# The head of a one-layer encoder block on one core: loads of x and of the first weights in another order, the z projection in pieces around the transposes, roots and low parts on other engines

## The reference

```python
def rmsnorm(x, g):
    y = x * lax.rsqrt(jnp.mean(x * x, axis=-1, keepdims=True) + EPS) * g

h = rmsnorm(x, norm_mix_g)
proj = h @ w_in        # attention q|k|v, DeltaNet q|k|v|z|a|b, two gates
ya = swa_sink_attention(aq, ak, av, ...)
yb = gated_deltanet(bq, bk, bv, bz, ba, bb, ...)   # conv + SiLU on q, k, v; SiLU(z) on the output
x = x + (sigmoid(ga) * (ya @ w_up_a) + sigmoid(gb) * (yb @ w_up_b)) @ w_out
x = x + memory_cross_attention(rmsnorm(x), rmsnorm(mem), ...)
x = x + hierarchical_moe(rmsnorm(x), ...)          # 32 experts, top 2 of the best group
return rmsnorm(x, norm_final_g)
```

## Time and profile before

| | us |
|---|---|
| median of 3 runs | 805.44 (804.22 to 806.6) |
| the profiled execution, its own time | 806.24 |
| its span | 804.4 |
| busy in the span: PE, PEld | 748.4, 598.3 |
| busy in the span: DVE, ACT, POOL | 341.6, 256.1, 300.7 |

### The profile page before, as it was taken

One profiled execution on the slowest core, in us unless ns is written; L12 is line 12 of the kernel. 1 busy time (PEld: TensorE's weight loads), 2 busy tenths in 40 slices (PEclk: granted clock), 3 DMA queues, 4 the chain that ended last, 5 costly groups with the idle time before them and its releaser, 6 DMA issues.

```text
span 804.4 us, 14079 instructions
## 1 busy us (share of the span) xinstructions
PE 748.4 (93%) x5523; PEld 598.3 (74%) x5523; DVE 341.6 (42%) x805; ACT 256.1 (32%) x462; POOL 300.7 (37%) x346
## 2 busy tenths in 40 slices
PE   5999999999999999999999999979999999988784
PEld 5887788788878877888888887857767776665551
DVE  6466643285684861435415333651222112211125
ACT  5343232361633767322305255511111111111012
POOL 2774525441520452254444254333333333322111
PEclk9999999999999999999999999999999999999998
DMA  9956742510220522474385294499999999999975
GB/s 250 162 110 124 218 124 53 104 42 13 53 53 20 136 56 53 98 216 96 83 176 169 60 320 183 180 358 375 390 385 389 390 393 387 380 386 387 390 300 219
DMA packets 74346, 166.60 MB, mean 207 GB/s; under 512 B 18838, under 2 KB 46310, under 8 KB 66344
## 3 DMA queue, kind: packets, MB, share of 16 engines
q1 hardware_dynamic: 65856, 150.34, 58.9%
q0 software_dynamic: 5392, 9.61, 3.6%
q10 hardware_dynamic: 3032, 5.74, 2.3%
HBM read 156.98 MB, written 16.97 MB: 216 GB/s over the span
## 4 chain that ended last, share of the span: by engine, by line
PE 58%; DMA 26%; DVE 9%; issue 2%; POOL 2%; ACT 1%; SPq 1%; ACTq 0%; DVEq 0%; POOLq 0%
DMA arena<-in_w_exp_up 24%; PE bank L1075 13%; PE bank L1077 12%; PE bank L1076 12%; PE bank L1068 12%; PE bank L1424 3%; DMA arena<-y_half 1%; PE bank L1434 1%; PE bank L1116 1%; DVE rows L1864 1%; DVE rows L1863 1%; PE bank L1226 1%; DVE h_lo L1836 1%; DVE hT L1908 1%; DMA rt<-in_norm_ffn_g 1%
## 5 line engine op out<-in xcount | busy, mean ns | idle before, releaser
L876 POOL TENSOR_TENSOR ring_low<-ring,w_high 128x512 fp32r<-128x512 f32 (+1 forms) x64 | 81.4, 1272 | 117.2 <-ACT w_high L1516 113.1
L1075 PE MATMUL bank<-h_hi,w_high 128*128 128x512 f32 x296 | 119.5, 404 | 0.0
L1076 PE MATMUL bank<-h_lo,w_high 128*128 128x512 f32 x296 | 115.8, 391 | 0.0
L1424 PEld LDWEIGHTS bank<-arena,hT 128*64 128x64 f32 x1728 | 96.6, 136 | 24.7 <-issue 12.5
L1424 PE MATMUL bank<-arena,hT 128*64 128x128 f32 x1728 | 100.7, 274 | 8.7 <-DMA arena<-in_w_exp_up 6.7
L876 POOL TENSOR_TENSOR w_low<-ring,w_high 128x512 fp32r<-128x512 f32 x56 | 75.9, 1355 | 59.1 <-ACT w_high L1516 54.9
L2182 DVE SCALAR_TENSOR_TENSOR rt<-rt,bank 128x128 f32<-128x128 f32 x32 | 9.2, 288 | 175.3 <-ACT rt L1749 175.3
L1516 ACT ACTIVATE w_high<-ring 128x2048 fp32r<-128x2048 f32 (+1 forms) x32 | 58.7, 1836 | 58.5 <-PE bank L1077 39.3
L1077 PE MATMUL bank<-h_hi,ring_low 128*128 128x512 f32 x168 | 66.6, 396 | 0.0
L1075 PEld LDWEIGHTS bank<-h_hi,w_high 128*128 128x128 f32 x296 | 55.7, 188 | 14.5 <-issue 3.5
L1076 PEld LDWEIGHTS bank<-h_lo,w_high 128*128 128x128 f32 x296 | 55.7, 188 | 11.0
(11 more groups left out here) (330 smaller groups left out, 1313.8 us busy)
## 6 DMA issues: line engine op xcount, KB each, us to landing
arena<-in_w_exp_gate SPq DMA_DIRECT2D x27, 1024.0 KB, 13.3
arena<-in_w_exp_up SPq DMA_DIRECT2D x27, 1024.0 KB, 17.0
arena<-in_w_exp_down SPq DMA_DIRECT2D x27, 1024.0 KB, 19.2
ring<-in_w_in SPq DMA_DIRECT2D x33, 512.0 KB, 6.6
ring<-in_w_exp_gate SPq DMA_DIRECT2D x5, 1024.0 KB, 13.8
ring<-in_w_exp_up SPq DMA_DIRECT2D x5, 1024.0 KB, 17.3
ring<-in_w_exp_down SPq DMA_DIRECT2D x5, 1024.0 KB, 20.5
xres<-in_x SPq DMA_DIRECT2D x8, 512.0 KB, 7.2
```

Of the source, the lines that this page charges most:

```text
L876: after(pool.tensor_tensor(low, full, high, ALU.subtract), w_lo if kk == KD - 2 else step["pool"])
L1075: pe.matmul(o, l_hi, r_hi, start=(n == 0), stop=False)
L1076: pe.matmul(o, l_hi, r_lo, start=False, stop=False)
L1424: ins = pe.matmul(bank[CAP * half:CAP * half + CAP, 1, P * n:P * n + P], xgT[:, x, kk, :], w[:, kk, P * half:P * half + P], start=(kk == 0 ...
```

## The change

- SP issues the loads as x tile 0, first half of the lead, x tile 1, second half of the lead, x tiles 2 and 3, chunks 1 and 2.
- The first two z jobs become four: `("zp",0)`, which does high by high of tile 0 between the transposes of tiles 0 and 1; `("zp",1)`, the rest of tile 0 and high by high and high by low of tile 1, between the transposes of tiles 1 and 2; `("z",0,0)`, low by high of tile 1; `("z",0,1)`, all of tiles 2 and 3 in six passes of 8 matmuls, the low parts of h last. The first three share a bank.
- The root of tile 1 moves from DVE to POOL (six instructions with a power in place of twelve). DVE makes the roots of tiles 2 and 3 after the gains of tile 1.
- POOL no longer waits for the diagonals. Its `h_lo` of tile 0 comes between the lead's low parts; `h_lo` of tile 1 and the low part of chunk 1 come next, `h_lo` of tiles 2 and 3 after those. ACT makes the high part of chunk 1 after `h_hi` of tile 1.
- DVE makes `h_lo` of tiles 0 and 1 as each tile's gains are done, of 2 and 3 after all gains.

```diff
+    turned = [[("hT", "mix", t, q) for q in range(2)] for t in range(NT)]
+    jobs = [("vec",)] + turned[0] + [("zp", 0)] + turned[1] + [("zp", 1)] + turned[2] + turned[3]
...
@@ sync
-            for t in range(NT):
+            def load_x(t):
                 sp.dma_start(xres[:, t, :], x[0, t * P:(t + 1) * P, :]).then_inc(x_in[t], 16)
+            load_x(0)
...
                     sp.dma_start(lead_dst[:, 0:4], lead_src[:, 0:4]).then_inc(lead_in, 16)
+                    load_x(1)
...
+                if n == 0:
+                    load_x(2)
+                    load_x(3)
...
@@ gpsimd
-            pool.wait_ge(diag_ready, NT)
             for n in range(4):
                 s = slice(n * CHUNK_W // 4, (n + 1) * CHUNK_W // 4)
+                if n == 1:
+                    v, y, y2 = var[:, 1:2], rstd[:, 1:2], newton[:, 1:2]
+                    pool.wait_ge(squared, 2)
+                    after(pool.tensor_scalar(v, squares[:, 1:2], 1.0 / D, EPS, ALU.mult, ALU.add))
+                    after(pool.tensor_tensor(y, v, neg_half, ALU.pow))
...
+                    after(pool.tensor_tensor(y, y, y2, ALU.mult), mix_rstd)
+                if n == 2:
+                    low_of_hT("mix", 0)
...
-            for t in range(NT):
+            low_of_hT("mix", 1)
+            low_part(1)
+            for t in range(2, NT):
                 low_of_hT("mix", t)
...
@@ tensor
+                    order = {("zp", 0): [(0, h_hi, 0)], ("zp", 1): [(0, h_lo, 0), (0, h_hi, 1), (1, h_hi, 0), (1, h_hi, 1)], ("z", 0, 0): [(1, h_lo, 0)],
+                             ("z", 0, 1): [(2, h_hi, 0), (2, h_hi, 1), (3, h_hi, 0), (3, h_hi, 1), (2, h_lo, 0), (3, h_lo, 0)]}[job]
...
@@ scalar
+                    square(0)
+                    lead_high(0, lead_in, 16, lead_hi)
+                    square(1)
+                    lead_high(1, chunk_in[0], 32, w_hi)
+                    high_of_hT(phase, 0)
+                    square(2)
+                    square(3)
+                    high_of_hT(phase, 1)
+                    high_part(1)
+                    high_of_hT(phase, 2)
+                    high_of_hT(phase, 3)
...
@@ vector
-            for t, count in ((0, 1), (1, 1), (2, 2)):
-                rms(t, count)
...
+                    if phase == "mix" and q == 1:
+                        if t == 0:
+                            dve.wait_ge(mix_rstd, 1)
+                            diagonal_of(1)
+                            low_of_hT(phase, 0)
+                        if t == 1:
+                            rms(2, 2)
+                            diagonal_of(2)
+                            diagonal_of(3)
+                            low_of_hT(phase, 1)
+                        if t == NT - 1:
+                            low_of_hT(phase, 2)
+                            low_of_hT(phase, 3)
```

More of the change, by code:

```diff
@@ L1154, in emit, with part @@
                     return ins
[L1155 to L1169, removed]
+                if k == "zp" or k == "z" and job[1] == 0:
+                    def part(t, h_of, w_of):
+                        pe.wait_ge(h_hi_ready["mix"], 2 * t + 1)
+                        if h_of is h_lo:
+                            pe.wait_ge(h_lo_ready["mix"], t + 1)
+                            pe.wait_ge(pool_lo_ready["mix"], t + 1)
+                        for kk in range(KD):
+                            if kk == KD // 2:
+                                pe.wait_ge(h_hi_ready["mix"], 2 * t + 2)
+                            if kk in (0, KD // 2):
+                                pe.wait_ge(*((w_lo, 1) if w_of else (w_hi, 1) if kk else (lead_hi, 1)))
+                            ins = pe.matmul(o[:, 256 * (t % 2):256 * (t % 2) + 256], h_of[:, kk, t * P:(t + 1) * P], w_parts(split_chunks[0], kk, 0, 256)[w_of],
+                                            start=(kk == 0 and h_of is h_hi and not w_of and t % 2 == 0), stop=(kk == KD - 1 and (h_of is h_lo if t else w_of == 1)), skip_group_check=True)
+                        return ins
+                    order = {("zp", 0): [(0, h_hi, 0)], ("zp", 1): [(0, h_lo, 0), (0, h_hi, 1), (1, h_hi, 0), (1, h_hi, 1)], ("z", 0, 0): [(1, h_lo, 0)],
+                             ("z", 0, 1): [(2, h_hi, 0), (2, h_hi, 1), (3, h_hi, 0), (3, h_hi, 1), (2, h_lo, 0), (3, h_lo, 0)]}[job]
+                    for one in order:
+                        ins = part(*one)
@@ L1537, in norm_rows, with square @@
                 base = NORM_TILES[phase]
-                for t in range(tiles):
+                def square(t):
                     dst = rows[:, t % 2, :] if phase != "mem" else o_flat
@@ L1542, in norm_rows, with lead_high @@
                     after(nc.scalar.activation(dst, source(t), ACT.Square, accum_out=squares[:, base + t:base + t + 1]), squared)
+                def lead_high(half, landed_on, n, ready):
+                    s = slice(half * CHUNK_W // 2, (half + 1) * CHUNK_W // 2)
+                    act.wait_ge(landed_on, n)
+                    copy(w_high[:, 0, s], chunk(split_chunks[0])[:, s], ready)
                 if phase == "mix":
-                    lead = chunk(split_chunks[0])
-                    for half, (landed_on, n, ready) in enumerate(((lead_in, 16, lead_hi), (chunk_in[0], 32, w_hi))):
-                        s = slice(half * CHUNK_W // 2, (half + 1) * CHUNK_W // 2)
-                        act.wait_ge(landed_on, n)
-                        copy(w_high[:, 0, s], lead[:, s], ready)
-                    for t in range(tiles):
-                        high_of_hT(phase, t)
+                    square(0)
[9 more added lines that the diff above has]
+                    high_of_hT(phase, 3)
                     return
+                for t in range(tiles):
+                    square(t)
                 act.wait_ge(rstd_ready, 1)
@@ L1567, in _ @@
                 c = job[-1]
-                if job in high_at:
+                if job in high_at and job != ("z", 0, 0):
                     high_part(high_at[job])
@@ L1808, in _, with diagonal_of @@
             after(nc.vector.memset(one, 1.0))
-            for t, count in ((0, 1), (1, 1), (2, 2)):
-                rms(t, count)
-                if t == 0:
-                    dve.wait_ge(first_in, FIRST)
-                for tile in range(t, t + count):
-                    after(ts(diag[:, tile], ident, rstd[:, tile:tile + 1], None, ALU.mult), diag_ready)
+            def diagonal_of(tile):
+                after(ts(diag[:, tile], ident, rstd[:, tile:tile + 1], None, ALU.mult), diag_ready)
+            rms(0, 1)
+            dve.wait_ge(first_in, FIRST)
+            diagonal_of(0)
             gain_slots = gain_e.rearrange("p (k o) -> p k o", o=1).to_broadcast([P, KD, CAP])
```

24 lines of the change are left out of this document (12 added, 12 removed).

## The result

The changed kernel takes 810.76 us (median of 5 runs, 810.09 to 811.91), the kernel before 805.44 (5 runs, 804.14 to 806.6): ratio 1.0062, 95% interval 1.0046 to 1.0078. It is slower, by 5.3 us where 1.6 were forecast, and 0.5 us outside the range. The profiled execution has a span of 810.1 us and a time of 811.91.

The account below looks back on a forecast made before the run. PE is full from the first conv matmul at 32.88 us on, so only the head before it could shorten. Conv was put at 34.5, +1.6 on the median 805.44, giving 807.0 us; range 803.0 to 810.3.

Parts of the forecast that it names:

- the pause of POOL: POOL waits for chunk 1's high part, 19.6 to 20.8 us; seven DVE instructions pass at full pace from 19.4.
- The loads: Start of the head: lead's first half at 7.5 us, x tile 1 8.8, second half 11.0, x tile 3 13.0.
- a sign: Check in the new profile: ACT's first copy of the lead at 7 to 8 us.
- PE up to the third tile: PE in the head: tile 0 turned by 12.0 us, tile 1 by 16.4, `("zp",1)` ended at 21.2.
- The deciding step: DVE's root of tiles 2 and 3, slowed beside POOL: PE waits from 21.2 to 23.8, 2.6 us.
- two DVE instructions for each of POOL's: Rule for DVE's root beside POOL: about two small DVE instructions get through per POOL instruction.
- My bound for this term: +2.1 us if one DVE instruction passes per POOL instruction, or chunk 1's low parts start right at the root.
- Rival 2: PE falls to the slow pace in its wait and turns tiles 2 and 3 slowly: +3.7, 809.1 us; chance 0.24.
- The rest of z: PE after the diagonals: tiles 2 and 3 turned by 27.4 us, `("z",0,0)` by 28.3, z ended about 34.5.
- Rival 1: Two-column DVE instructions may pass POOL unhindered, so the head shrinks: z ends at 31.0, -1.9, 803.5 us; chance 0.24.
- The pass-through of the head: What moves the first conv matmul, at 32.88 us before, moves the kernel's end by as much.

Follow-up runs that it names:

- e5: The kernel before the change with POOL's wait for the four diagonals deleted, so its low parts start earlier; 807.84 us.
- e2: The changed kernel with 39 matmuls that nobody reads put into PE's wait before the transposes of tile 2; 810.80 us.
- e10: The changed kernel with 33 matmuls that nobody reads put into PE's wait before the transposes of tile 2; 810.53 us.
- e1: The changed kernel with POOL held until all four diagonals are made, before its h_lo of tile 1; 807.07 us.
- e4: The changed kernel with POOL's low part of chunk 1 moved behind h_lo of tiles 2 and 3; 809.22 us.
- e9: The kernel of e3 with 11 early matmuls that nobody reads on PE, from the landing of x tile 0; 805.93 us.
- e3: The changed kernel with the root of tiles 2 and 3 on POOL, lead's low parts before h_lo of tile 0, ACT's squares reordered; 805.42 us.
- e6: The kernel before the change with only the new order of SP's loads and of ACT's squares and copies; 809.63 us.

## Why the prediction was wrong

Sign, place and mechanism were right; the sum was short by 4.0 us at the conv (34.5 forecast, 38.51 measured). The step that failed is the pause of POOL in which most of the root was to pass.

- **The loads**: nearly right. ACT copies the lead's second half from 10.92 on and squares x tile 1 from 8.70 on, near the 11.0 and 8.8 of the forecast. Its first copy starts at 6.23 instead of 7.5, before the 7 to 8 that I had named as a sign; that is why POOL's first low part came so early (7.44).
- **PE up to the third tile**: 0.9 us late. PE's transposes began at 9.48 instead of 8.63. Of these 0.85 us, 0.5 are the small vectors, which landed for PE at 8.76 instead of 8.24, and 0.32 are PE's wait for the diagonal: POOL's first low part, which I let start "at 8.6" beside nothing, ran into the end of DVE's first root. Tile 0 then took 3.7 us instead of 3.4. `("zp",1)` ended at 22.1 instead of 21.2.
- **The deciding step**: this is the one that failed. The rule "two DVE instructions for each of POOL's" held; e5 shows it in eight instructions. The pause it was applied to did not. I let POOL stand still from 19.6 to 20.8 and seven instructions pass "at full pace from 19.4 to 20.8", the first of them already beside h_lo. POOL's h_lo of tile 1 ran until 20.39: POOL's chain was 0.8 late, as its h_lo of tile 0 had waited until 14.93 for ACT's h_hi, which I had ready at 13.65. Chunk 1's high part, on the other side of the pause, was done on time, 18.92 + 1.92 = 20.84. So the pause was 0.62 us instead of 1.2, and three instructions passed instead of seven. The four others cost two more of POOL's instructions, 2 x 1.34 = 2.7 us, and diagonal 2 released PE at 26.50 instead of 23.8. My bound for this term was +2.1. A pause between two chains with different upstream delays can vanish; I had the estimate of its ends from two such chains and gave neither an error.
- **Rival 2, the slow pace**, is what came, though I gave it 0.24 against 0.42 for the forecast without it. Its sum was the forecast's +1.6 and 2.1 for the pace; measured, the pace cost 5.22 us for 32 transposes instead of 3.6, +1.6. That it came from the wait, e2 and e10 show.
- **The rest of z**: 6.79 us instead of 7.1, -0.3. The sum 2.7 + 1.6 - 0.3 = 4.0.
- **Rival 1** is refuted: instructions of one and two columns are held up as those of 16 and 32 are. With POOL off the root, DVE needs 2.99 us (e1).
- **The pass-through of the head** held for the change itself (+5.63 at the conv, +5.7 in span, +5.3 in the medians), and up to the experts it holds in every profiled execution but e4's. The medians of e9 and e10 do not show their heads' gains of 1.2 and 1.4 us, so to the end 1:1 is not shown in both directions.

## What to carry to other kernels

Before letting an engine start earlier, look at what runs beside it. Narrow VectorE instructions in a chain on the critical path (here twelve of 0.16 us for a root) multiply beside GpSimd's two-operand work, one in two of them taking a whole GpSimd instruction; put such a chain where GpSimd stands still, or give it to GpSimd itself (e3). When a forecast rests on a gap between two chains, work it out once with the gap and once without; and when the sum has a long wait on TensorE, give it with the slow pace behind it and without: here it came after 4.25 and 2.25 us and not after 3.50 and 2.48. Before a gain of 1 us is looked for in a time of 805, find out how much the rest of the kernel scatters from execution to execution.

## What the runs showed of the hardware

- A VectorE instruction over one column (7.52 us, 1.19 long) or two is stopped by GpSimd's 128x512 with two operands, where it takes 0.16 alone; the wide h_lo goes from 0.69 to between 1.45 and 1.67. A power root on two columns costs GpSimd 2.1 us (18.02 to 20.12 in e3).
- TensorE's granted clock fell after 4.25 us of standing still (0.50 in 27.3 to 30.6, after) and after 2.25 us (0.50 in 36.5 to 39.8, e4). Both times it still read 1.00 in the first 0.7 and 1.2 us in which TensorE worked again. It did not fall after 3.50 us in e5 or after 2.48 in e6: both then turned 32 transposes in 3.84 us, at 1.00. So the length of the wait alone does not tell; these runs don't settle what else does.
- At the start the pace was also half in all kernels without early matmuls, though the granted clock reads 1.00 in the profile's views. The traces' records of that clock start later: at 13.56 us in the changed kernel, 18.97 in e3, 19.18 in e1, 10.66 in e9. Up to there the pace was slow (tile 1 took 3.14 and 3.29 us in e3 and e1, 1.95 in the changed kernel), so a 1.00 ahead of the first record says nothing. Earlier work on TensorE takes the slow pace up.
- Behind the conv all these kernels have nearly the same work, and what their profiled executions differ in lies in the experts' stage: 264.7 to 269.2 us from its start to the end, against 505.2 to 505.6 from the conv to its start (507.1 in e4).
